# Group norm of a Mamba-2 layer: channel sums on every lane, root and reciprocal on 128x512, in place of tokens on lanes and a spreading matmul

## The reference, cut to what matters

```
def gated_group_rms_norm(y, z, g):
    u = y * silu(z)
    u = u.reshape(..., 8, 256)
    u = u * rsqrt(mean(u * u, axis=-1) + 1e-5)
    return u.reshape(...) * g
...
y = gated_group_rms_norm(y, z, gate_norm_g)
return x + y @ w_out
```

## Time and profile before

| | us |
|---|---|
| median of 3 runs | 2302.6 (2297.57 to 2309.23) |
| the profiled execution, its own time | 2302.14 |
| its span in the profile | 2300.3 |
| PE busy | 1991.0 |
| DVE busy | 1359.8 |
| ACT busy | 888.6 |
| POOL busy | 441.6 |

### The profile page before, as it was taken

The page is one execution under the profiler, slowest core; times in us unless marked ns, Lnnn a source line. Parts: engine busy times, 40 slices in busy tenths (PEclk is TensorE's granted clock), DMA queues, the critical chain, the costliest instruction groups (busy, mean ns, idle before and its releaser), DMA issues.

```text
span 2300.3 us, 28354 instructions
## 1 busy us (share of the span) xinstructions
PE 1991.0 (87%) x9576; PEld 1597.2 (69%) x9576; DVE 1359.8 (59%) x1770; ACT 888.6 (39%) x1439; POOL 441.6 (19%) x324
## 2 busy tenths in 40 slices
PE   0466999999999968999999986999999979995457
PEld 0344878888887745788888875888888858883235
DVE  8888344334347687544344468676677545238983
ACT  1355343323234245433233332454455422235550
POOL 3754120000034010300000343132122240001003
PEclk9788999999999979999999998999999989997778
DMA  3111223232332200333233321222222213230002
GB/s 148 25 25 25 92 91 99 93 100 92 100 94 90 83 19 12 96 94 100 91 100 93 99 81 48 73 65 68 78 67 65 74 46 93 90 98 13 0 0 73
DMA packets 54079, 166.32 MB, mean 72 GB/s; under 512 B 13168, under 2 KB 13168, under 8 KB 53488
## 3 DMA queue, kind: packets, MB, share of 16 engines
q1 hardware_dynamic: 54000, 165.28, 22.8%
HBM read 160.80 MB, written 2.10 MB: 71 GB/s over the span
## 4 chain that ended last, share of the span: by engine, by line
PE 72%; DVE 16%; ACT 4%; POOL 3%; issue 3%; DMA 3%; DVEq 0%; POOLq 0%; SPq 0%; ACTq 0%; PEldq 0%
PE bank L182 16%; PE bank L184 16%; PE bank L183 16%; PE bank L1360 3%; PE bank L1361 3%; PE bank L1362 3%; DMA raw<-in_w_dram 2%; PE bank L1386 1%; PE bank L684 1%; PE bank L1394 1%; PE bank L1388 1%; PE bank L1387 1%; DVE R L2060 1%; DVE S L2045 1%; DVE s2t_mx L2046 1%
## 5 line engine op out<-in xcount | busy, mean ns | idle before, releaser
L201 DVE TENSOR_TENSOR w_lo<-raw,w_hi 128x1024 fp32r<-128x1024 f32 x289 | 374.4, 1296 | 537.1 <-ACT w_hi L193 535.5
L193 ACT ACTIVATE w_hi<-raw 128x1024 fp32r<-128x1024 f32 x289 | 306.2, 1060 | 765.0 <-DMA raw<-in_w_dram 764.9
L182 PE MATMUL bank<-x1h,w_hi 128*128 128x512 f32 x936 | 367.6, 393 | 10.6 <-DVE x1l L216 8.8
L184 PE MATMUL bank<-x1h,w_lo 128*128 128x512 f32 x936 | 365.1, 390 | 0.0
L183 PE MATMUL bank<-x1l,w_hi 128*128 128x512 f32 x936 | 365.0, 390 | 0.0
L182 PE MATMUL bank<-x0h,w_hi 128*128 128x512 f32 x832 | 328.9, 395 | 0.0
L184 PE MATMUL bank<-x0h,w_lo 128*128 128x512 f32 x832 | 324.2, 390 | 0.0
L183 PE MATMUL bank<-x0l,w_hi 128*128 128x512 f32 x832 | 323.9, 389 | 0.0
L230 POOL TENSOR_TENSOR sq<-h 128x512 f32 (+1 forms) x72 | 86.9, 1207 | 861.4 <-DVEq L803 659.4
L182 PEld LDWEIGHTS bank<-x1h,w_hi 128*128 128x128 f32 x936 | 176.2, 188 | 50.6 <-DVE x1l L216 10.9
L183 PEld LDWEIGHTS bank<-x1l,w_hi 128*128 128x128 f32 x936 | 176.2, 188 | 37.2 <-issue 1.0
(11 more groups left out here) (385 smaller groups left out, 3044.7 us busy)
## 6 DMA issues: line engine op xcount, KB each, us to landing
raw<-in_w_dram SPq DMA_DIRECT2D x289, 512.0 KB, 3.5
h<-in_xT_dram SPq DMA_DIRECT2D x1, 2048.0 KB, 9.1
Ur<-in_xu_dram SPq DMA_DIRECT2D x8, 256.0 KB, 2.6
out_dram<-h SPq DMA_DIRECT2D x8, 256.0 KB, 2.1
const<-in_const_dram SPq DMA_DIRECT2D x1, 1425.0 KB, 12.0
B_st<-in_B_dram SPq DMA_DIRECT2D x1, 1024.0 KB, 13.9
C_st<-in_C_dram SPq DMA_DIRECT2D x1, 1024.0 KB, 15.9
p_in<-in_pT_dram SPq DMA_DIRECT2D x1, 1024.0 KB, 4.8
```

What stands on the lines that cost most here:

```text
L182: e.matmul(b, w_hi[:, w, k], xh[:, k], start=(k == 0), stop=False)
L184: last = e.matmul(b, w_lo[:, w, k], xh[:, k], start=False, stop=(k == KT - 1))
L193: e.activation(w_hi[:, z], raw[:, z], ACT.Copy).then_inc(hi_split, 1)
L201: e.tensor_tensor(w_lo[:, z], raw[:, z], w_hi[:, z].bitcast(F32), ALU.subtract).then_inc(w_split, 1)
```

## The change

The squares become the moving operand and a full 128x128 block of ones the stationary one: two matmuls of 128x512, accumulated in bank 6. Every lane then holds every token's sum. ACT takes the root of 128x512 into the buffer `sd`, DVE takes the reciprocal of 128x512 in place, and yg reads `sd` in SBUF where it read bank 3 in PSUM. The spreading matmul, its semaphore and the two small buffers are gone. Nothing is moved to another slot. The root now waits for the yg of the group before, since `sd` is read there.

```diff
--- before.py
+++ after.py
@@ -1217,7 +1217,6 @@
         at = [own]
         T4 = own_buf("T4", [5, CHUNKS, HEADS])
         ea = own_buf("ea", [HEADS])
-        sd4, rg4 = own_buf("sd4", [CHUNKS]), own_buf("rg4", [CHUNKS])
         pre = own_buf("pre", [2, TOK + 3])
         cv = own_buf("cv", [2, TOK])
         xt = own_buf("xt", [2, 2, TOK])
@@ -1323,7 +1322,6 @@
         ssd_turned = Steps(sem("ssd_turned"), "tx0 tx1 tb")
         ssd_products = Steps(sem("ssd_products"), "cb a0 a1 n1 a2 n2 a3 y0 y1 y2 y3")
         ssd_sums = Steps(sem("ssd_sums"), "sum")
-        ssd_spread = Steps(sem("ssd_spread"), "R")
         ssd_inputs = Steps(sem("ssd_inputs"), "xd0 xd1 cbm")
         ssd_gaps = Steps(sem("ssd_gaps"), "m0 m1 m2 m3")
         ssd_states = Steps(sem("ssd_states"), "S1 Sm2 S2 Sm3 S3")
@@ -1477,22 +1475,11 @@
                 e.wait_ge(ssd_gaps.sem, ssd_gaps.at("m3", p))
                 e.wait_ge(ssd_exps.sem, ssd_exps.at("x3", p))
                 e.wait_ge(ssd_squares.sem, ssd_squares.at("q1", p))
-                for c in range(CHUNKS):
-                    for i in range(2):
-                        last = e.matmul(bank[6][:, c:c + 1], usq[:, i, c * LANES:(c + 1) * LANES], C("ones", hi=1), start=(i == 0), stop=(i == 1))
-                ssd_sums.took("sum", last)
-            elif k == 2:
-                e.wait_ge(ssd_normed.sem, ssd_normed.at("rg", p))
-                if p < GROUPS - 1:
-                    e.wait_ge(ssd_inputs.sem, ssd_inputs.at("xd1", p + 1))
-                else:
-                    e.wait_ge(ssd_states.sem, ssd_states.at("S3", p))
-                for c in range(CHUNKS):
-                    last = e.matmul(bank[3][:, c * LANES:(c + 1) * LANES], rg4[:, c:c + 1].to_broadcast([LANES, LANES]), C("ident"), start=True, stop=True)
-                ssd_spread.took("R", last)
+                e.matmul(bk[6], C("ones"), usq[:, 0], start=True, stop=False)
+                ssd_sums.took("sum", e.matmul(bk[6], C("ones"), usq[:, 1], start=False, stop=True))
 
         def mamba_tensor(e):
-            for counters in (ssd_turned, ssd_products, ssd_sums, ssd_spread):
+            for counters in (ssd_turned, ssd_products, ssd_sums):
                 counters.open(e)
             pe_unit(e, U_DT, 0, 0, x1h, x1l, ready(x_ready, 56))
             for n in range(SLOTS):
@@ -1620,17 +1607,16 @@
                     ssd_skipped.took(f"ud{i}", e.scalar_tensor_tensor(uu[:, i], xt[:, p % 2, i], par[:, d0:d0 + 1], bk[4 + i], ALU.mult, ALU.add))
             elif k == 2:
                 e.wait_ge(ssd_roots.sem, ssd_roots.at("sd", p))
-                e.wait_ge(ssd_spread.sem, ssd_spread.before("R", p))
-                ssd_normed.took("rg", e.reciprocal(rg4[:, :], sd4[:, :]))
+                ssd_normed.took("rg", e.reciprocal(sd[:, :], sd[:, :]))
             if k == (2 if p == GROUPS - 1 else 3):
                 tail_yg(e, p)
 
         def tail_yg(e, p):
-            e.wait_ge(ssd_spread.sem, ssd_spread.at("R", p))
+            e.wait_ge(ssd_normed.sem, ssd_normed.at("rg", p))
             e.wait_ge(ssd_squares.sem, ssd_squares.at("q1", p))
             for i in range(2):
                 g0 = PC["gate_g"][0] + 2 * p + i
-                ssd_normed.took(f"yg{i}", e.scalar_tensor_tensor(uu[:, i], uu[:, i], par[:, g0:g0 + 1], bk[3], ALU.mult, ALU.mult))
+                ssd_normed.took(f"yg{i}", e.scalar_tensor_tensor(uu[:, i], uu[:, i], par[:, g0:g0 + 1], sd[:, :], ALU.mult, ALU.mult))
 
         def dt_vector(e, n):
             tt, ts, stt = e.tensor_tensor, e.tensor_scalar, e.scalar_tensor_tensor
@@ -1754,8 +1740,8 @@
                     ssd_squares.took(f"q{i}", e.activation(usq[:, i], uu[:, i], ACT.Square))
             elif k == 2:
                 e.wait_ge(ssd_sums.sem, ssd_sums.at("sum", p))
-                e.wait_ge(ssd_normed.sem, ssd_normed.before("rg", p))
-                ssd_roots.took("sd", e.activation(sd4[:, :], bank[6][:, 0:CHUNKS], ACT.Sqrt, bias=eps5[:, :], scale=1.0 / 256))
+                e.wait_ge(ssd_normed.sem, ssd_normed.before("yg1", p))
+                ssd_roots.took("sd", e.activation(sd[:, :], bk[6], ACT.Sqrt, bias=eps5[:, :], scale=1.0 / 256))
             if k == (2 if p == GROUPS - 1 else 3):
                 if p == 4:
                     e.wait_ge(unit_done, U_MAMBA + OUT_AT[0] + 4)
```

## The result

The kernel after takes 2325.36 us, the kernel before 2306.74 (medians of nine runs each): ratio 1.0081, interval 1.0067 to 1.0094, so 18.6 us slower. The profiled execution of after took 2327.79 us, its span 2325.9, which is 25.6 more than before. It is one of the slower executions of after, 2.4 us above its median, so the profiles show a little more than the 18.6 us between the medians. Of the 25.6, 5.1 lie ahead of the first tail, in code that is the same in both: the transposes of xt that open the stretch start at 1474.49 us before and at 1479.60 after. From their end to the end of the first sums of the layer behind the Mamba layer (L236) it is 423.3 us before and 444.2 after. The 20.9 us between are what has to be explained.

A forecast was written before the change was run, and what follows sets the result against it. It took DVE's unbroken 33 us behind the reciprocal, which makes PE wait, as the place to price. Input slots 9.0, output slots 4.0 and last tail 1.4 gave +14.4 on 2302.1: forecast 2316.5 us, range 2302 to 2328.

The forecast's parts named there:

- The sums on PE: Norm matmuls on PE: wide sums add 0.08 us per group, the dropped spreading saves 0.89, so PE saves 0.81.
- Reciprocal and root: Widening to 128x512: root on ACT +0.44 us, reciprocal on DVE +3.18, so DVE behind them comes 3.6 us later.
- yg: On DVE, reading its operand from SBUF instead of PSUM was taken to change nothing: zero.
- Added waits: The root's wait for the previous group's yg and PE's a1 waiting for the root: both free, the latter by 1 us.
- Input slots: Tails p = 0, 1, 3, 4, 5: late DVE makes PE's chunk 3 2.4 us late, net +1.8 per group, +9.0 in all.
- DVE against POOL: Input slots, the unknown: convolution steps meeting POOL instructions; 1.9 us loss might go, or 1.3 us more be added.
- The third rival: Slower still: PE's clock drops in input groups and POOL costs more, 4.4 us per group, 2332 us; chance 15%.
- Output slots: Tails p = 2, 6: PE waits for DVE's add to `h`, +1.45 us each plus 0.55 for the clock, +4.0 together.
- Last tail: Tail p = 7: yg starts 0.95 us later, PE idles over 5 us, 0.45 added for slow stretch, together +1.4.
- the one in which PE sets the time: Rival at PE's queue, reciprocal covered: -0.81 us per group, 2296 us; chance 7%.
- The one in which the input slots swallow it all: Rival: the POOL meeting gets cheaper, input slots cost nothing, only the other three tails cost: 2306 us; chance 20%.

The follow-up runs named there:

- e1: The changed kernel with root and reciprocal on 128x4 only, so all but four tokens lack the inverse root: 2293.69 us, ratio 0.9957 against before.
- e3: The changed kernel with the reciprocal placed later on DVE, behind the mask, the split and the convolution of its slot: 2298.86 us, ratio 0.9978 against before.
- e2: The kernel before with one 128x512 reciprocal added behind the small one, on a buffer nothing reads: 2320.59 us, ratio 1.0067 against before.
- e4: The changed kernel with the reciprocal on 128x256, half its width, the root kept whole: 2306.67 us, ratio 1.0002 against before.
- e5: The changed kernel with ACT making x3, which POOL's cs of chunk 3 needs, ahead of ACT's exponential step e3: 2318.72 us, ratio 1.0063 against before.
- e6: The changed kernel with the inverse root made on ACT by Ln and Exp, without root or DVE reciprocal: 2294.77 us, ratio 0.9949 against before.
- after_again: The changed kernel run once more, unaltered, for a second profile: 2321.05 us, ratio 1.0074 against before.

## Why the prediction was right, and where its sizes were off

The forecast was 2316.5 in a range of 2302 to 2328, slower at 0.56. The kernel is slower by 0.67 to 0.94%, and the time lies in the range, 9 us above the forecast. The cause is the forecast's, and so are places and releasers. Four us of the nine are the runs of before themselves, whose median rose from 2302.6 to 2306.7 with six more runs. The rest is in the sizes. Part of the closeness is luck: the meetings of DVE and POOL changed in two ways that nearly cancel (below), and p = 6 came out under its term while p = 2 and p = 5 came out well over theirs.

- *The sums on PE.* Right. From the transposes to a0 the first tail takes 0.9 us less (14.94 for 15.84), for the predicted 0.81. e1 shows the saving whole, since DVE is not late there.
- *Reciprocal and root.* Right: 3.35 us for the predicted 3.36, and 0.70 for the root.
- *yg.* Right, zero. The Trainium skill's 62 cycles for a PSUM source ("VectorE: DVE Perf Modes", TRN2 errata) would, by estimate, leave some 680 ns for the SBUF form. 744 were measured, so the trace decides against it, as the prediction had it.
- *Added waits.* Right. a1 has no bracket in any input tail; the sixteen records of a0 and a1 (1494.54) run through at 1.95 us, as before.
- *Input slots.* The mechanism was right, link by link; the size of 1.8 us per group was small, 2.3 on average. Measured from the transposes at the head of each group, m3 starts 3.92 us later (38.70 against 34.78), not 3.6; e3 3.78, not 3.4; c3 ends 3.75 later, not 3.4; PE begins chunk 3 2.92 late, not 2.4. The wait of 0.62 us ahead of the transposes was swallowed as said, and with it what their start behind a wait had cost on top (their records now overlap what is ahead of them), together 0.84. That gives 2.92 - 0.84 = 2.08 for p = 0. Of the half microsecond by which chunk 3 was later than forecast, 0.17 is the root's start, which hangs on the load ahead of it, and 0.15 to 0.2 is DVE against POOL; the rest is not placed.
- *DVE against POOL.* This was the term called unknown, with ends of 1.9 us less and 1.3 more. It came out near nothing, but by two changes that nearly cancel: x0l (1503.17 to 1506.68) costs two convolution steps 1.1 us (2.57 in the rows above) in place of 1.9, and c1 (from 1508.04, 1.29 us) now costs the third 1.1 (1.83 for 0.75). The rule of the Trainium skill cited in the prediction ("SBUF — State Buffer", "Who interferes with whom") agrees with the second meeting: c1, which starts 0.01 us earlier, is not held up, and the convolution step ends as late as if it had waited for most of c1.
- *PE's clock in the input slots.* The third rival had given it a part, the forecast none. It fell in one input tail of this profile, p = 5, which is 1.5 of the 3.99 us that this tail costs: from the start of chunk 3 to the end of the transposes behind it 9.2 us passed (1798.27 to 1807.50), where the first tail took 7.7. The granted clock of that group's stretch was 0.97, where the two first groups had 1.00. In the second profile of after it was p = 5 again, and p = 1. The wait is the same 1.28 us in all five, so the length of that wait alone does not decide it.
- *Output slots.* Here the step that gave 2.0 us each failed, for p = 2. It took the root's start as given. The root of this tail started 13.35 us behind the end of the transposes, before 11.53, because the weight load that ACT handles ahead of it took 5.26 us, where the same row of the chain has 3.65 and 3.53 in the two tails before it. The add came 5.4 us later, 1.8 of them from the root's start. PE idled 4.04 us, not 2.2, and then ran nine matmuls at a start to start of 0.43 us, not 0.23, the lower of the two clock levels. So PE's unit starts 19.84 us behind the transposes, before 16.45 (1586.54), and takes 7.8 us, before 5.6: 3.4 us for the wait and 2.2 for the clock. The chain has this load in both profiles of after:

```profile
1584.98 5.26 DMA raw<-in_w_dram
...
1592.63 0.70 ACT sd L1744
```

  In e3's profile it took 3.74 us and in e2's 3.62, and these kernels waited 0.80 and 1.14 us in slot 26; in e4's and e5's it took 4.73 and 4.70, with waits of 1.91 and 3.49. What makes it slow in some kernels was not found, and no kernel was made to tell it. The distance from the load issued before it does not settle it: that is 6.38 us in after, e4 and e5, and 7.1 to 7.2 in before, e1, e3 and e6, but it is 6.38 in e2 too, where the load took 3.62. For p = 6 there is no such load. The wait was 1.46 us, the granted clock stayed at 1.00, and the tail cost 1.47: the term of 1.45 without what was counted for the clock.
- *Last tail.* Right in its mechanism: 1.01 us for the 0.95 of yg, and the wait is 5.41 us where "over 5" was written. Another 1.16 us lie between this unit and L236, where 0.45 had been added for the clock; what they consist of was not worked out.

Of the rivals, the one in which PE sets the time is what e1, e3 and e6 show in the input slots once the wide reciprocal is out of the way, at 0.9957, 0.9978 and 0.9949: it had the saving right (e1 is 10 us faster, 6.5 were worked out) and the cover wrong. The one in which the input slots swallow it all needed a cheaper meeting with POOL, which the two changes above did not give.

## What to carry to other kernels

An instruction made longer costs what stands unbroken behind it on its engine, up to the first gap, less the slack of whoever waits there; a long idle time in front of it pays for nothing, unless work from behind is moved into it, as e3 did: the same instructions, and no cost left in the input tails. When an exact rewrite takes work from the bounding engine and makes a short operation on another one wide, look for an engine with a gap at that very place: with the inverse root on ACT the same change is a gain of 0.5%. And read a group's waits by their sum and by the starts around them, since one wait may keep its length whatever the delay.

## What the runs showed of the hardware that was not expected

- A bracket tells less than the wait costs. In the first tail PE's four brackets add up to 3.06 us and the saving is 0.9, yet chunk 3 starts 2.92 late, not 2.2: each start behind a wait cost 0.2 us on top, on average (m0's records take 1.16 us and not 1.05, and the distances between starts grow with them).
- The granted clock fell behind waits of 0.50 to 0.77 and 1.28 us, one matmul group apart, in three of the ten such tails of after's two profiles, and cost 1.5 us each time. In e2 it did so in one of five, in e4 and e5 in none. Nor does the length of a single wait for `xt` decide it: at the same place the next 8 us had a granted clock of 1.00 behind 2.81 us (e6) and of 0.79 behind 2.79 us (after_again).
- The reciprocal takes 3.35 us for 128x512, 1.75 for 128x256 (e4) and 0.18 for 128x4, where a two-input operation of DVE on 128x512 takes 0.68 to 0.75; Ln and Exp on ACT take 0.69 and 0.63.
- DVE and POOL held each other up where DVE read two wide tensors from SBUF: a convolution step of 0.75 us took 1.83 beside POOL's 1.29 us `cs`. The evacuation `zs`, one of whose two wide operands lies in PSUM, took its usual 0.69 us beside POOL's `uu` (1521.19 us in before, POOL busy from 1520.76 for 2.52).
- A load of weights took 5.26 us at one place in both profiles of one kernel and 3.6 to 4.7 at the same place in others; this stays open.
